# Early modulation on unsplit float32 weights, and one group of late modulation moved to the feed-forward head

## The chip, the cores and the metric

One core of a Trainium2 chip runs one launch of the kernel. The metric is device time in microseconds (us), lower is better. All inputs lie in the chip's memory (HBM); all arithmetic is on values of 32 bits.

## The reference, cut to what matters

One layer of a streaming encoder, for 512 prompt positions and 32 sample positions, 544 columns in all, with a width of 2048:

```
mod = silu(c) @ w_mod + b_mod          # 2048 x 12288 weights, two rows of c (prompt, sample)
sh_a, sc_a, gt_a, sh_f, sc_f, gt_f = split(mod, 6)
h   = rmsnorm(x, g_attn) * (1 + sc_a) + sh_a
z   = h @ w_in                         # then two kinds of attention on z
x   = x + gt_a * (concat(A, B) @ w_out)
h2  = rmsnorm(x, g_ffn) * (1 + sc_f) + sh_f
u   = causal_conv3(h2 @ w_up);  y = silu(u_gate) * u_val
x   = x + gt_f * (y @ w_down)
out = rmsnorm(x, g_final)
```

Every one of the six parts of mod has 2048 numbers for each of the two rows of c.

## The kernel before

x is held transposed, features on the 128 partitions, in 16 tiles `xT[:, kt, :]` of 128 x 544. The large products are computed from operands that are split in two parts of the type float32r: `w_hi` is a copy of a weight chunk in that type (ScalarE, `hi`, L828), `w_lo` the rest (VectorE, `lo`, L1194), and `products` (L1590 to L1592) adds three matmuls, hi x hi, hi x lo and lo x hi. A weight chunk is 128 x 1024 numbers, 512 KB. Each is loaded by a transfer of SyncE's queue into one of four slots `w_raw`, in the order of the table `STREAM`; `slot_free` makes SyncE wait until the chunk that was four places earlier in the table has been used. So all stages share one ring of four slots.

The program has these stages:

- **The early stage.** 64 chunks `("e", e)` of w_mod, 8 for each of 8 groups of 512 columns, give sh_a and sc_a, which h needs. Each chunk is split like all others; the four columns of `c_parts` (hi and lo parts of silu(c), two rows) are the stationary operand and the chunk is streamed, 4 matmuls of 512 columns for a chunk (L1564). After a group, `group_out` (ScalarE) copies its row, `group_columns` (PE, L1548) turns it into columns and `group_mod` (VectorE) adds the bias. From chunk `X_AT` = 8 on PE also transposes x (L1579, L1580), 5 transposes after each of 16 chunks. POOL squares xT (L614), VectorE sums the squares, PE sums over the partitions, and POOL then multiplies each xT tile by the reciprocal root (L627) and applies scale and shift to tiles 0 to 11 (L622); ScalarE does that for the last four tiles (L849). `h_hi` and `h_lo` split h into `x_hi` and `x_lo`. The table `NORM_AT` puts one tile's `h_hi` and `h_lo` between every second chunk's `hi` and `lo`.
- **z and attention.** 72 half slabs of z on PE, with the attention between them.
- **The output projection**, 32 halves, and at its end the second norm.
- **The feed-forward head**: the first `GRP` = 4 of 44 feed-forward tiles (`hidden` with `has_down` false, jj = 0 to 3). They have no `down` products yet. Then a **loop** over the other tiles, and a tail.

The other 64 tiles of mod (gt_a, sh_f, sc_f, gt_f) are the **late modulation**: 16 groups of 8 chunks. They use no matmul for the product: VectorE multiplies and adds for the prompt (`late_sum`, L1285, two instructions of 128 x 512 for a chunk), ScalarE multiplies for the sample (`late_mul`, L887, two) and POOL adds (`late_add`, L724, two). PE only sums over the partitions at a group's end (`late_tile`, L1601). Ten groups lie in the z stage, four (`LATE2`) in the output projection, two (`LATE3`) in the head; only gt_f, needed from the loop on, is in the head.

In the head, VectorE's order for tile jj of 1 to 3 is: `lo` of one weight chunk, two late chunks, `lo` of the second, two late chunks, the convolution of the gate half, then two `lo` for the next tile's first products. For jj = 0, four late chunks stand together after the first convolution. ScalarE starts each tile (`hidden`) with a wait for PE's first half of it (`u_done`), and only then makes that tile's third chunk's `w_hi`. Before the loop SyncE waits until all four slots are free.

Of the kernel before, what the change touches and what calls it, by code (L numbers as in the profile page):

```python
# [36 lines left out]
P = 128  # L37
# [185 lines left out]
SUM_AT = X_AT + KT + 2  # L223
LAG = NW
NORM_AT = {34 + 2 * k if k < 8 else 57 + 2 * (k - 8): k for k in range(12)}
# [5 lines left out]
LATE2 = 4 * LPG  # L231
LATE3 = 2 * LPG
# [24 lines left out]
STREAM = [("e", _e) for _e in range(EC)] + [("w", 0), ("w", 1)]  # L257
# [40 lines left out]
SC0 = EC + FC0  # L298
# [6 lines left out]
def build(nc, A, O):  # L305
# [5 lines left out]
    with ctx:  # L311
# [34 lines left out]
        c_parts = on(st0, "c_parts", [P, KT, 4], F32R)  # L346
        mod_rows = [on(st0, f"mod_rows{i}", [P, EG]) for i in range(2)]
        pair = on(st0, "pair", [P, 2])
# [90 lines left out]
        ld_c, c_hi, c_lo = sem("ld_c"), sem("c_hi"), sem("c_lo")  # L439
        e_ev, e_t, e_tev = sem("e_ev"), sem("e_t"), sem("e_tev")  # L440
# [136 lines left out]
        def _(pool):  # L577
# [14 lines left out]
            pool.wait_ge(consts, 4)  # L592
            pool.tensor_tensor(pair[0:4, :], ident[0:4, 0:2], ident[0:4, 2:4], ALU.add).then_inc(consts, 1)

# [1263 lines left out]
```

## Time and profile before

| | before |
|---|---|
| median of 3 runs | 2742.48 us (2741.48 to 2748.51) |
| profiled execution | 2740.53 us, span 2738.8 us |
| PE busy | 2592.2 us, 95% of the span |
| VectorE (DVE) busy | 1641.2 us, 60% |
| ScalarE (ACT) busy | 1010.4 us, 37% |
| GpSimd (POOL) busy | 643.4 us, 23% |
| mean granted TensorE clock | 0.976 of full speed |
| moved by DMA | 324.94 MB |

The span runs from the first to the last instruction. A busy PE is not a PE at its peak: matmuls overlap, so what one costs in a row of them is the distance from its start to the next one's start. PEld is the load of a stationary operand and lies beside PE. A granted clock of 1.00 is 2.4 GHz, of 0.50 it is 1.2 GHz. A matmul on plain float32 stands in the trace as two records, one on float32r and a transpose as one.

### The profile page before, as it was taken

Reading aid. Unit: us, or ns where it says so; the run is one execution under the profiler, and the core shown is the slowest. Engines: PE = TensorE matmul, PEld = TensorE weight load, DVE = VectorE, ACT = ScalarE, POOL = GpSimd, SP = SyncE. Lnnn points to the kernel's source line nnn. Section 1 sums busy time; section 2 is a strip of 40 time slices with the busy share of each in tenths; the row PEclk is TensorE's granted clock in tenths of the full one; section 3 lists DMA queues with packets and bytes.
Section 4 is the critical chain, followed back from the end, with each engine's and each line's share of the span. In section 5 each row is a group of like instructions: output and inputs, shape, how many; then the busy total and the mean of one; then the engine's idle time right before and its main releaser. Section 6 shows DMA issues by size and latency. Waiting matters only on the chain.

```text
span 2738.8 us, 50324 instructions
## 1 busy us (share of the span) xinstructions
PE 2592.2 (95%) x19815; PEld 2452.4 (90%) x19815; DVE 1641.2 (60%) x2890; ACT 1010.4 (37%) x2015; POOL 643.4 (23%) x534
## 2 busy tenths in 40 slices
PE   5679999999998997799999999999999999999997
PEld 2258889888988997799999999999999999999997
DVE  5889889974446887864444454445444544444454
ACT  4556666664344335432222222222222222222224
POOL 3777777771002543510000000000000000000003
PEclk8799999999999998999999999999999999999998
DMA  8766556562224663443322333232232332332331
GB/s 290 240 210 181 186 176 181 181 169 63 57 56 138 170 175 91 140 123 93 92 79 79 93 93 87 84 94 87 84 89 83 93 92 78 94 91 80 92 94 69
DMA packets 416208, 324.94 MB, mean 119 GB/s; under 512 B 44410, under 2 KB 360218, under 8 KB 414880
## 3 DMA queue, kind: packets, MB, share of 16 engines
q1 hardware_dynamic: 410032, 302.55, 37.5%
q0 software_dynamic: 5248, 14.56, 1.7%
q10 hardware_dynamic: 688, 4.47, 0.4%
q8 instruction: 169, 2.77, 0.4%
q14 instruction: 71, 0.58, 0.1%
HBM read 307.67 MB, written 14.07 MB: 117 GB/s over the span
## 4 chain that ended last, share of the span: by engine, by line
PE 77%; DVE 8%; POOL 4%; issue 4%; DMA 3%; ACT 2%; SPq 1%; ACTq 0%; POOLq 0%; DVEq 0%
PE ps L1590 24%; PE ps L1592 23%; PE ps L1591 23%; DVE late_f L1285 3%; PE ps L1679 2%; PE ps L1645 2%; DMA w_raw<-in_w_out 2%; DMA w_raw<-in_w_mod 1%; POOL oT L724 1%; POOL xT L622 1%; ACT w_hi L828 1%; DVE w_lo L1194 1%; POOL xT L627 1%; DVE oT L1285 1%; PE ps L1663 1%
## 5 line engine op out<-in xcount | busy, mean ns | idle before, releaser
L1590 PE MATMUL ps<-x_hi,w_hi 128*128 128x272 f32 x4480 | 1317.2, 294 | 45.3 <-DVE w_lo L1194 25.0
L1592 PE MATMUL ps<-x_hi,w_lo 128*128 128x272 f32 x4480 | 1302.9, 291 | 0.0
L1591 PE MATMUL ps<-x_lo,w_hi 128*128 128x272 f32 x4480 | 1292.9, 289 | 0.0
L1590 PEld LDWEIGHTS ps<-x_hi,w_hi 128*128 128x128 f32 x4480 | 849.7, 190 | 62.4 <-issue 28.1
L1591 PEld LDWEIGHTS ps<-x_lo,w_hi 128*128 128x128 f32 x4480 | 851.1, 190 | 0.0
L1592 PEld LDWEIGHTS ps<-x_hi,w_lo 128*128 128x128 f32 x4480 | 848.5, 189 | 0.0
L1194 DVE TENSOR_TENSOR w_lo<-w_raw,w_hi 128x1024 fp32r<-128x1024 f32 x432 | 546.3, 1292 | 346.8 <-ACT w_hi L828 345.8
L828 ACT ACTIVATE w_hi<-w_raw 128x1024 fp32r<-128x1024 f32 x432 | 441.8, 1056 | 745.1 <-PE ps L1592 561.6
L1591 PE MATMUL ps<-y_lo,w_hi 128*128 128x272 f32 x1408 | 407.3, 289 | 0.0
L1590 PE MATMUL ps<-y_hi,w_hi 128*128 128x272 f32 x1408 | 405.7, 288 | 0.0
L1592 PE MATMUL ps<-y_hi,w_lo 128*128 128x272 f32 x1408 | 405.0, 288 | 0.0
L783 POOL TENSOR_TENSOR ext<-cv 128x544 f32<-128x544 f32 x1 | 1.5, 1517 | 1476.2 <-ACT cv L1091 1476.2
L1041 ACT ACTIVATE ext<-ps 128x272 f32<-128x272 f32 (+2 forms) x264 | 74.0, 317 | 528.2 <-PE ps L1592 527.7
L1590 PEld LDWEIGHTS ps<-y_hi,w_hi 128*128 128x128 f32 x1408 | 265.6, 189 | 0.1
L1592 PEld LDWEIGHTS ps<-y_hi,w_lo 128*128 128x128 f32 x1408 | 264.8, 188 | 0.0
L1591 PEld LDWEIGHTS ps<-y_lo,w_hi 128*128 128x128 f32 x1408 | 264.6, 188 | 0.0
L1387 DVE SCALAR_TENSOR_TENSOR x<-ps,mod,x 128x272 f32<-128x272 f32 (+2 forms) x576 | 207.6, 400 | 92.4 <-PE ps L1592 92.3
L1431 DVE COPY ext<-cols 128x2 f32 (+1 forms) x88 | 14.9, 169 | 400.8 <-ACT ext L1041 400.8
L724 POOL TENSOR_TENSOR oT<-oT 128x512 f32<-128x512 f32 x150 | 224.3, 1495 | 31.7 <-ACT oT L887 23.8
L1285 DVE SCALAR_TENSOR_TENSOR oT<-w_raw,cs,oT 128x512 f32<-128x512 f32 x150 | 179.3, 1195 | 2.8
L724 POOL TENSOR_TENSOR late_f<-late_f 128x512 f32<-128x512 f32 x90 | 140.9, 1565 | 143.1 <-ACT late_f L887 134.3
L1285 DVE SCALAR_TENSOR_TENSOR late_f<-w_raw,cs,late_f 128x512 f32<-128x512 f32 x90 | 128.0, 1422 | 3.1
(201 smaller groups left out, 2182.6 us busy)
## 6 DMA issues: line engine op xcount, KB each, us to landing
w_raw<-in_w_mod SPq DMA_DIRECT2D x192, 512.0 KB, 4.6
w_raw<-in_w_up SPq DMA_DIRECT2D x176, 512.0 KB, 4.8
w_raw<-in_w_down SPq DMA_DIRECT2D x88, 512.0 KB, 4.4
w_raw<-in_w_in SPq DMA_DIRECT2D x56, 512.0 KB, 3.9
w_raw<-in_w_in SPq DMA_DIRECT2D x32, 256.0 KB, 3.7
w_raw<-in_w_out SPq DMA_DIRECT2D x16, 512.0 KB, 5.3
w_raw<-in_w_out SPq DMA_DIRECT2D x64, 128.0 KB, 4.0
x_transposed<-xT SPq DMA_DIRECT2D x4, 1088.0 KB, 5.9
```

What stands on the lines that cost most here:

```text
L622: ins = pool.tensor_scalar(xT[:, kt, a:a + c], xT[:, kt, a:a + c], mod[:, SC_A + kt, g:g + 1], mod[:, SH_A + kt, g:g + 1], ALU.mult, ALU.add)
L724: ins = pool.tensor_tensor(acc, late_prod(n, 0) if p == 0 and k == 1 else acc, late_prod(n, k), ALU.add)
L828: act.activation(w_hi[c % NW][:, :], w_raw[raw][:, :], ACT.Copy).then_inc(s_hi, 1)
L1041: ins = act.activation(ext[x][:, a + 2 + 2 * g:a + 2 + 2 * g + n], bank(2 * x + h)[:, a - HALF[h][0]:a - HALF[h][0] + n], ACT.Copy)
L1194: dve.tensor_tensor(w_lo[c % NW][:, :], w_raw[raw][:, :], w_hi[c % NW][:, :].bitcast(F32), ALU.subtract).then_inc(s_lo, 1)
L1285: ins = dve.scalar_tensor_tensor(out=acc_d(g), in0=w, scalar=c, in1=acc_d(g), op0=ALU.mult, op1=ALU.add)
L1387: ins = dve.scalar_tensor_tensor(out=x1[:, n, a:a + m], in0=b[:, a - HALF[h][0]:a - HALF[h][0] + m], scalar=mod[:, gate + n, g:g + 1], in1 ...
L1590: pe.matmul(out[:, 0:n], hi_w, hi_x, start=first, stop=False)
L1591: pe.matmul(out[:, 0:n], hi_w, lo_x, start=False, stop=False)
L1592: return pe.matmul(out[:, 0:n], lo_w, hi_x, start=False, stop=last)
L1645: mm = pe.matmul(S[t % 2][0:np_, pc:pc + n], zq[qi % 2][r, q0:q0 + np_], kk, start=True, stop=True)
L1679: mm = pe.matmul(B7[0:np_, oc:oc + vn], probsT[0:n, tc:tc + np_], v, start=first, stop=last)
```

## The change

In the early stage:

- The chunks of w_mod are no longer split. PE multiplies `w_raw` itself, as float32, with the two columns of `cs` = silu(c) as the stationary operand: 2 float32 matmuls of 512 columns for a chunk (4 records) in the place of 4 float32r ones. 64 `hi` and 64 `lo` fall away, and SyncE frees a slot when PE has used the chunk (`m_used`), not when `lo` has.
- `group_columns` transposes rows of 2, and no longer sums pairs of 4, one record for each of 32 tiles where there were two.
- POOL's part of the norm is gone. ScalarE squares each transposed tile out of PSUM. VectorE's `h_mul` multiplies by scale and reciprocal root in one instruction, ScalarE's `h_hi` adds the shift and writes `x_hi`, and VectorE's `h_lo` adds the shift again and subtracts `x_hi`. Each of the three has two pieces for a tile, 512 prompt and 32 sample columns.
- In `STREAM` the two first chunks of w_in stand ahead of the last two of w_mod.

In the late modulation one group of 8 chunks moves: `LATE2` falls from 4 to 3 groups and `LATE3` rises from 2 to 3. A tile of the head now has 6 late chunks instead of 4.

```diff
-SUM_AT = X_AT + KT + 2
-LAG = NW
-NORM_AT = {34 + 2 * k if k < 8 else 57 + 2 * (k - 8): k for k in range(12)}
+SUM_AT = X_AT + KT + 4
+W_AT = 62
...
-LATE2 = 4 * LPG
-LATE3 = 2 * LPG
+LATE2 = 3 * LPG
+LATE3 = 3 * LPG
...
-STREAM = [("e", _e) for _e in range(EC)] + [("w", 0), ("w", 1)]
+STREAM = [("e", _e) for _e in range(W_AT)] + [("w", 0), ("w", 1)] + [("e", _e) for _e in range(W_AT, EC)]
...
-        HEAD_LATE[_j, _q] = [LATE1 + LATE2 + 4 * _j + 2 * _q + _i for _i in range(2)]
+        HEAD_LATE[_j, _q] = [LATE1 + LATE2 + 6 * _j + 3 * _q + _i for _i in range(3)]
...
-                if old[0] != "mod":
-                    sp.wait_ge(s_lo, old[1] + 1 + (EC if old[0] == "w" else 0))
+                if old[0] == "w":
+                    sp.wait_ge(s_lo, old[1] + 1)
+                elif old[0] == "e":
+                    sp.wait_ge(m_used, old[1] + 1)
...
+            def h_hi(kt):
+
+                act.wait_ge(n_mul, kt + 1)
+                for a, c, g in ((0, TP, 0), (TP, TS, 1)):
+                    ins = act.activation(x_hi[:, kt, a:a + c], xT[:, kt, a:a + c], ACT.Identity,
+                                         bias=mod[:, SH_A + kt, g:g + 1])
+                ins.then_inc(n_hi, 1)
...
+            def h_mul(kt):
+
+                for a, c, g in ((0, TP, 0), (TP, TS, 1)):
+                    ins = dve.scalar_tensor_tensor(out=xT[:, kt, a:a + c], in0=xT[:, kt, a:a + c],
+                                                   scalar=mod[:, SC_A + kt, g:g + 1], in1=n0_rstd[:, a:a + c],
+                                                   op0=ALU.mult, op1=ALU.mult)
+                ins.then_inc(n_mul, 1)
...
+            for q in range(4):
+                for g in range(max(3, 2 * q), 2 * q + 2):
+                    if g == E_GROUPS - 1:
+                        lo(0, RAW_OF[("w", 0)] % NR, 0)
+                        lo(1, RAW_OF[("w", 1)] % NR, 1)
+                    group_mod(g)
+                dve.wait_ge(mod_ok, q + 1)
+                for kt in range(EGT * q, EGT * q + EGT):
+                    h_mul(kt)
+                    if kt >= 2:
+                        h_lo(kt - 2)
+            h_lo(KT - 2)
+            h_lo(KT - 1)
...
-                pe.wait_ge(s_lo, e + 1)
+                raw = RAW_OF[("e", e)] % NR
+                pe.wait_ge(ld_raw[raw], LOADED[("e", e)])
                 for k in range(EK):
                     kt = EK * (e % EPG) + k
-                    for part in (w_hi, w_lo):
-                        mm = pe.matmul(bank(7 - g % 2)[0:4, :], c_parts[:, kt, :], part[e % NW][:, EG * k:EG * k + EG],
-                                       start=(kt == 0 and part is w_hi), stop=(kt == KT - 1 and part is w_lo))
+                    mm = pe.matmul(bank(7 - g % 2)[0:2, :], cs[:, kt, :], w_raw[raw][:, EG * k:EG * k + EG],
+                                   start=kt == 0, stop=kt == KT - 1)
                 mm.then_inc(m_used, 1)
```

PE's queue where the transposes of x begin, before: chunk 8 of w_mod, the 5 transposes of one x tile, and the next chunk.

```order
L1564 MATMUL ps<-w_hi,c_parts 4x512
L1564 MATMUL ps<-w_lo,c_parts 4x512
L1564 MATMUL ps<-w_hi,c_parts 4x512
L1564 MATMUL ps<-w_lo,c_parts 4x512
L1579 MATMUL ps<-ident,x_nat 128x128 x4
L1580 MATMUL ps<-ident,x_nat 128x32
L1564 MATMUL ps<-w_hi,c_parts 4x512
L1564 MATMUL ps<-w_lo,c_parts 4x512
```

The same place of PE's queue after the change; the first row holds chunks 6, 7 and 8.

```order
L1539 MATMUL ps<-w_raw,cs 2x512 x6
L1556 MATMUL ps<-ident,x_nat 128x128 x4
L1557 MATMUL ps<-ident,x_nat 128x32
L1539 MATMUL ps<-w_raw,cs 2x512 x2
L1523 MATMUL ps<-ident,mod_rows 128x2 x4
L1556 MATMUL ps<-ident,x_nat 128x128 x4
```

The matmuls read the loaded chunk and wait for no split; group 0's columns are made two chunks after its end, not four.

VectorE's queue at the end of the early stage, after the change: groups 6 and 7 of mod with the two splits of w_in's first chunks between them, then the last norm tiles.

```order
L1164 TENSOR_TENSOR mod<-ps,cols 128x4 x2
L1155 TENSOR_TENSOR w_lo<-w_raw,w_hi 128x1024 x2
L1164 TENSOR_TENSOR mod<-ps,cols 128x4 x2
L1126 SCALAR_TENSOR_TENSOR mod<-mod,cols 128x4 x2
L1174 SCALAR_TENSOR_TENSOR xT<-xT,mod,n_rstd 128x512
L1174 SCALAR_TENSOR_TENSOR xT<-xT,mod,n_rstd 128x32
L1183 SCALAR_TENSOR_TENSOR x_lo<-xT,mod,x_hi 128x512
L1183 SCALAR_TENSOR_TENSOR x_lo<-xT,mod,x_hi 128x32
```

Before, four single `x_lo` instructions of 128x544 stood behind group 7; now four `h_mul` and six `h_lo`, two pieces each, stand behind it.

VectorE's queue in the head, tiles jj = 0 and 1, before:

```order
L1285 SCALAR_TENSOR_TENSOR late_f<-w_raw,cs,late_f 128x512 x7
L1194 TENSOR_TENSOR w_lo<-w_raw,w_hi 128x1024 x2
...
L1194 TENSOR_TENSOR w_lo<-w_raw,w_hi 128x1024
L1285 SCALAR_TENSOR_TENSOR late_f<-w_raw,cs,late_f 128x512 x4
L1194 TENSOR_TENSOR w_lo<-w_raw,w_hi 128x1024
L1285 SCALAR_TENSOR_TENSOR late_f<-w_raw,cs,late_f 128x512 x4
L1431 COPY ext<-cols 128x2
```

The same rows after the change:

```order
L1261 SCALAR_TENSOR_TENSOR late_f<-w_raw,cs,late_f 128x512 x11
L1155 TENSOR_TENSOR w_lo<-w_raw,w_hi 128x1024 x2
...
L1155 TENSOR_TENSOR w_lo<-w_raw,w_hi 128x1024
L1261 SCALAR_TENSOR_TENSOR late_f<-w_raw,cs,late_f 128x512 x4
L1258 TENSOR_SCALAR late_f<-w_raw,cs 128x512
L1261 SCALAR_TENSOR_TENSOR late_f<-w_raw,cs,late_f 128x512
L1155 TENSOR_TENSOR w_lo<-w_raw,w_hi 128x1024
L1261 SCALAR_TENSOR_TENSOR late_f<-w_raw,cs,late_f 128x512 x6
L1407 COPY ext<-cols 128x2
```

Four more instructions of 128 x 512 stand ahead of the `w_lo` pair that the next tile's first products wait for, in tile 0 and in every other tile of the head.

## Rows read from the trace of the kernel before

**Rows 1.** Busy time by stretch: length, PE, PEld, DVE, ACT, POOL, clock, DMA share, GB/s
```profile
88.00:174.00 86.00, 56.93 (x194) 18.95 (x192) 70.27 (x64) 48.48 (x56) 71.79 (x42) 0.81 0.74 224
856.00:1057.00 201.00, 192.73 (x1504) 190.28 (x1504) 160.56 (x185) 71.69 (x95) 91.78 (x60) 0.99 0.63 175
1097.00:1200.00 103.00, 85.07 (x659) 83.93 (x657) 86.27 (x89) 44.01 (x77) 49.07 (x30) 0.95 0.48 137
```

**Rows 2.** Groups by line, 0 to 175 us: busy, mean ns | idle before, releaser
```profile
L828 ACT ACTIVATE w_hi<-w_raw 128x1024 fp32r<-128x1024 f32 x66 | 68.3, 1051 | 53.0 <-DMA w_raw<-in_w_mod 51.3 <-DMA w_raw<-in_w_in 1.3 <-PE ps L1564 0.4
L1564 PE MATMUL ps<-w_hi,c_parts 128*4 128x512 f32 x128 | 61.6, 482 | 55.8 <-DVE w_lo L1194 55.6
```

**Rows 3.** Timeline of the norm in the early stage: start, us, engine, line
```profile
107.31 1.35 POOL L627 TENSOR_TENSOR xT<-xT,n_rstd 128x544 f32<-128x544 f32 x1
108.84 3.50 POOL L622 TENSOR_SCALAR xT<-xT,mod 128x512 f32<-128x512 f32 x2 [0.18 <-POOL xT L627]
112.31 1.36 POOL L627 TENSOR_TENSOR xT<-xT,n_rstd 128x544 f32<-128x544 f32 x1
```

**Rows 4.** Timeline, z stage: one float32 matmul of 512 columns, and what follows it
```profile
249.05 1.04 PE L1645 MATMUL ps<-past_kT,zq 64*32 64x512 f32 x2
249.93 0.22 PE L1645 MATMUL ps<-zk,zq 64*32 64x32 f32 x2
```

**Rows 5.** Timeline, the first transposes of x and the chunk behind them
```profile
38.07 0.60 PE L1579 MATMUL ps<-ident,x_nat 128*128 128x128 f32 x4
...
38.77 0.39 PE L1564 MATMUL ps<-w_hi,c_parts 128*4 128x512 f32 x1
...
39.00 0.39 PE L1564 MATMUL ps<-w_lo,c_parts 128*4 128x512 f32 x1
```

**Rows 6.** Transfers to 175 us: median us to landing of x's last; w_mod's, 90 to 120
```profile
x_nat<-in_x_sample ACTq DMA_DIRECT2D x1, 256.0 KB, 21.5
...
DMA to landing us min/median/max: 3.6/4.5/4.9
```

**Rows 7.** Timeline: last matmul of w_mod, the first of z, and the 49th of z
```profile
170.84 0.39 PE L1564 MATMUL ps<-w_lo,c_parts 128*4 128x512 f32 x1
...
174.27 0.39 PE L1590 MATMUL ps<-x_hi,w_hi 128*128 128x272 f32 x1
...
182.69 0.28 PE L1590 MATMUL ps<-x_hi,w_hi 128*128 128x272 f32 x1
```

**Rows 8.** All instructions of L1285 on `late_f`: ns min/median/max, first and last start
```profile
L1285 DVE SCALAR_TENSOR_TENSOR late_f<-w_raw,cs,late_f x90: 732/1592/1776, 859.2 to 1191.6; 128x512 f32<-128x512 f32 x90
```

**Rows 9.** Waits in the output projection, 856 to 1057 us: total, times, longest
```profile
PE ps L1590 <- DVE w_lo L1194: 6.8, 8, 2.6
```

**Rows 10.** Groups by line in the head, 1097 to 1200 us
```profile
L724 POOL TENSOR_TENSOR late_f<-late_f 128x512 f32<-128x512 f32 x30 | 49.1, 1636 | 48.1 <-ACT late_f L887 41.6 <-issue 3.7
L1285 DVE SCALAR_TENSOR_TENSOR late_f<-w_raw,cs,late_f 128x512 f32<-128x512 f32 x30 | 45.0, 1500 | 1.5
```

**Rows 11.** VectorE's timeline in the head, tiles 0 and 1
```profile
1102.73 9.97 DVE L1285 SCALAR_TENSOR_TENSOR late_f<-w_raw,cs,late_f 128x512 f32<-128x512 f32 x7
1112.62 2.35 DVE L1194 TENSOR_TENSOR w_lo<-w_raw,w_hi 128x1024 fp32r<-128x1024 f32 x2
...
1141.26 2.35 DVE L1194 TENSOR_TENSOR w_lo<-w_raw,w_hi 128x1024 fp32r<-128x1024 f32 x2
```

**Rows 12.** PE's waits at the starts of tiles 1, 2 and of the loop
```profile
1113.98 0.56 PE L1590 MATMUL ps<-x_hi,w_hi 128*128 128x272 f32 x1 [10.59 <-DVE w_lo L1194]
1142.62 0.36 PE L1590 MATMUL ps<-x_hi,w_hi 128*128 128x272 f32 x1 [1.10 <-DVE w_lo L1194]
1200.23 0.59 PE L1590 MATMUL ps<-x_hi,w_hi 128*128 128x272 f32 x1 [2.71 <-DVE w_lo L1194]
```

**Rows 13.** ScalarE's timeline: third weight chunk of tiles 1 and 2
```profile
1121.82 1.06 ACT L828 ACTIVATE w_hi<-w_raw 128x1024 fp32r<-128x1024 f32 x1 [2.90 <-PE ps L1592]
...
1148.91 1.06 ACT L828 ACTIVATE w_hi<-w_raw 128x1024 fp32r<-128x1024 f32 x1 [1.35 <-PE ps L1592]
```

More of the change, by code:

```diff
@@ L345, in build @@
         lam = [on(st0, f"lambda{i}", [P, A_DK]) for i in range(4)]
-        c_parts = on(st0, "c_parts", [P, KT, 4], F32R)
-        mod_rows = [on(st0, f"mod_rows{i}", [P, EG]) for i in range(2)]
-        pair = on(st0, "pair", [P, 2])
+        mod_rows = [on(st0, f"mod_rows{i}", [2, EG]) for i in range(2)]
         rows = on(st0, "rows", [P, 9, P])
@@ L871, in _ @@
                     act.wait_ge(lam_dot, 2)
                     act.activation(tiny[:, 4:6], tiny[:, 6:8], ACT.Exp).then_inc(lam_exp, 1)
-                if e == SUM_AT + LAG:
-                    root(0, n0_rstd[:, :])
-                if e in NORM_AT:
-                    h_hi(NORM_AT[e])
+            group_out(2)
+            root(0, n0_rstd[:, :])
+            for kt in range(EGT):
+                h_hi(kt)
+            group_out(3)
+            for kt in range(EGT, 2 * EGT):
+                h_hi(kt)
@@ L877, in late_mul @@
+            group_out(4)
+            group_out(5)
+            for kt in range(2 * EGT, 3 * EGT):
+                h_hi(kt)
+            group_out(6)
+            hi_early(0)
+            hi_early(1)
+            group_out(7)
+            for kt in range(3 * EGT, KT):
+                h_hi(kt)
             def late_mul(n):
@@ L1246, in _ @@
-            lo(0, RAW_OF[("w", 0)] % NR, EC)
-            lo(1, RAW_OF[("w", 1)] % NR, EC + 1)
-            group_mod(E_GROUPS - 1)
-            for kt in range(len(NORM_AT), KT):
-                h_lo(kt)
+                for a, c, g in ((0, TP, 0), (TP, TS, 1)):
+                    ins = dve.scalar_tensor_tensor(out=x_lo[:, kt, a:a + c], in0=xT[:, kt, a:a + c],
+                                                   scalar=mod[:, SH_A + kt, g:g + 1],
+                                                   in1=x_hi[:, kt, a:a + c].bitcast(F32), op0=ALU.add, op1=ALU.subtract)
@@ new lines, in h_lo @@
+                ins.then_inc(x_ok, 1)
+            dve.wait_ge(rows_t, len(ROW_COUNTS))
+            for i in range(1, len(ROW_COUNTS)):
+                row_out(i)
+            dve.wait_ge(ld_small, 80)
+            for i in range(2):
+                a, b = lam[2 * i], lam[2 * i + 1]
+                dve.tensor_tensor_reduce(a[:, :], a[:, :], b[:, :], 1.0, 0.0, ALU.mult, ALU.add,
+                                         tiny[:, 6 + i:7 + i]).then_inc(lam_dot, 1)
+            dve.wait_ge(rows_ev, len(ROW_COUNTS))
@@ new lines, in _ @@
+            group_mod(0)
+            for kt in range(1, KT):
+                dve.wait_ge(sq_mul, kt + 1)
+                if kt > 1:
+                    dve.wait_ge(sq_add, kt - 1)
+                ins = dve.tensor_tensor(n0_acc[:, :], n0_sq[0][:, :] if kt == 1 else n0_acc[:, :],
+                                        n0_sq[kt % 2][:, :], ALU.add)
+                ins.then_inc(sq_ok if kt == KT - 1 else sq_add, 1)
+            dve.wait_ge(lam_exp, 1)
+            step(dve.tensor_tensor(tiny[:, 3:4], tiny[:, 5:6], tiny[:, 4:5], ALU.subtract))
@@ L1546, in group_columns @@
                 for t in range(EGT):
[L1547 to L1549 removed]
+                    mm = pe.transpose(bank(5)[:, 2 * t:2 * t + 2], mod_rows[g % 2][0:2, P * t:P * t + P],
+                                      ident[0:2, 0:2])
                 mm.then_inc(e_t, 1)
[L1553 removed]
             for e in range(EC):
```

148 lines of the change are left out of this document (34 added, 114 removed).

## The prediction

> **What bounds the kernel now.** I read the busy time by stretch first, then for each stretch the change touches its groups and timeline. In the early stage nothing is full: from 88 to 174 us PE is busy 57 of 86 us at a granted clock of 0.81, and DMA moves 224 GB/s [rows 1]. PE waits 55.6 us for `w_lo` and ScalarE 51.3 us for weights [rows 2]. The releasers hide the cause. POOL needs 5.0 us for one tile of the norm, from one L627 to the next (107.31 to 112.31), and is never free in between [rows 3]. `NORM_AT` sets one tile against two chunks, and ScalarE and VectorE work in order; so over the 12 tiles that POOL scales, a chunk costs 2.5 us whatever DMA and PE could do.
>
> In the output projection PE is the bound, 192.7 of 201 us busy [rows 1], with 6.8 us of waits for `w_lo` [rows 9]. In the head it is not: 85.1 of 103 us busy, beside VectorE with 86.3 [rows 1]. 45.0 us of those are the 30 late instructions L1285 [rows 10], and tiles 1, 2 and the loop each start with PE waiting for a `w_lo`: 10.59, 1.10 and 2.71 us [rows 12]. What stands ahead of that `w_lo` in VectorE's queue are the late chunks [rows 11]. From the loop on PE is full, so a microsecond lost or won ahead of it stays.
>
> **Early stage: the chunks.** A float32 matmul of 512 columns costs 0.88 us at full clock, from 249.05 to 249.93 [rows 4]. The new chunk has two: 1.76 us, against four float32r ones of 0.23 (38.77 to 39.00 [rows 5]), 0.92. So PE's own work on the 64 chunks rises from 59 to 113 us, but the split, its waits and POOL's pace go. That row has 32 stationary columns and 64 rows, ours 2 and 128; I take the same price, since the number of streamed columns is the same. The five transposes of a tile of x take 0.70 us (38.07 to 38.77 [rows 5]).
>
> The start stays: the sample part of x lands 21.5 us after its issue at about 4 us [rows 6], and DMA is full until then. Both kernels should have used chunk 8 at about 38 us, where the first transposes of x stand now [rows 5]. From there the sum is 55 chunks x 1.76 = 96.8 us, 16 x 0.70 = 11.2, the sum of squares and 7 groups of columns about 5 (my estimate; the parts are 4 transposes each). That gives 151 us for the last matmul on w_mod, if PE never waits. DMA must give 512 KB in 1.76 us, about 298 GB/s; a slot's transfer lands in 4.5 us, and a slot has 3 x 1.76 = 5.3 us until PE is back [rows 6]. That holds by a small margin, so I add 4 us for waits and drops of the clock: 155 us, bounds 151 and 165, against 171.1 now (170.84 and one matmul [rows 7]). Squares and copies on ScalarE and the sums on VectorE lie beside this; a tile of x and a chunk leave them 2.46 us, and with POOL silent they have their short durations.
>
> **Early stage: the end.** Now z starts 3.4 us after the last matmul on w_mod and its first half of 48 matmuls ends at 182.7 us [rows 7]. The four last `x_lo` were short single instructions. After the change z can start at once, but `x_ok` for tiles 10 to 15 lies behind group 7's scale: copy, 4 transposes and the small sums 2.2 us, then four `h_mul` and six `h_lo` on VectorE. The minimum of L1285, two inputs and 512 columns, is 0.73 us [rows 8], which I read as the price without POOL's adds beside it; with the 32-column piece I take 0.95, an estimate. That is 2.2 + 9.5 + 0.4 = 12.1 us, longer than the matmuls of the half. So the first half of z ends at 155 + 12 = 167 us against 182.7: **15 us won**, with bounds 5 and 20. The 68 us of splits that ScalarE is rid of [rows 2] are no further gain: they lie beside PE's longer matmuls.
>
> A rule of the Trainium skill speaks against this. The row first: at 38.77 us, between two sets of transposes, the 512-column matmuls stand 0.23 us apart [rows 5], which is 2.4 GHz. "TensorE: Matmul & The Clock Gate", in "Part 4: PE-mode transpose", says that transposes do not count as work for the clock and that the full clock does not engage for them. By the row the stretch of 16 tiles costs 16 x 2.46 = 39 us; by the rule, taken for the whole stretch, it would run at 1.2 GHz and cost 78. The row decides here, as matmuls are most of the stretch.
>
> **Late modulation.** The moved group has 8 chunks, each with two instructions on VectorE, ScalarE and POOL, and one transfer on SyncE's queue. In the output projection these lay beside PE's products. What they give back is at most the 6.8 us of waits [rows 9] and part of ScalarE's and the gaps of `late_tile`; I take **3 us**, bounds 0 and 8.
>
> In the head they are on the path. Tile 0: seven L1285 take 9.97 us, then two `w_lo`, and PE starts at 1113.98 [rows 11, 12]. Two more chunks stand ahead of that. Tiles 1 to 3: the chain is PE's start, its first half, ScalarE's third chunk (1121.82 for tile 1 [rows 13]), `w_lo`, late chunks, `w_lo`, late chunks, convolution, the next `w_lo` pair, PE's start. It closes in 28.64 us, 1113.98 to 1142.62 [rows 12], where PE needs 192 matmuls and about 24. The slack of PE on this chain is the 1.10 us it waits; the work that hid the late chunks is used up. So every added chunk lengthens each tile by its time on VectorE: 2 x 1.5 = 3.0 us at the mean of the head [rows 10]. Two a tile, four tiles: 8 x 3.0 = 24 us. POOL does not set this, 6 x 2 x 1.64 = 19.7 us in a tile [rows 10]; nor ScalarE or DMA. Before the loop SyncE waits for all slots, and this wait moves by the same two chunks.
>
> Longer gaps also cool PE. From PE's start to the third chunk's `w_hi` tile 1, after a gap of 10.59 us, takes 7.84 us, tile 2, after 1.10 us, 6.29 [rows 12, 13]. That is 1.5 us for a cold start; I add it for two of the tiles, 3 us. **27 us lost.** Bounds: below 16 x 0.73 = 11.7 us, if each late instruction ran as without POOL [rows 8]; above 16 x 1.78 = 28.4 and a cold start at two places in each of four tiles, 6 x 1.5 more, 38. I take a value near the mean because POOL's adds run at the same time as now.
>
> **The sum**, against the profiled execution: 2740.5 - 15 - 3 + 27 = 2749.5 us. It lies 2 us under the median of the runs, so for a median 2751.5, rounded to 2752.
>
> **Rivals.** What a measurement can tell from no change here is about 0.3%, 8.2 us: slower begins at 2750.7, faster ends at 2734.3.
>
> 1. *The head takes the chunks more cheaply, no change.* With 18 us won ahead, the head must cost between 10 and 26 us, 1.2 to 3.3 us a chunk. For it: my sum without cold starts, 24 us, is already in this band. Against: the waits get longer, and chunks back to back meet POOL more often. Time at 20 us: 2744.
> 2. *The head has room, faster.* VectorE is busy 86 of 103 us [rows 1]; if its idle 17 us took most of the added 24, the head would cost 7 us and the result be 2731. It decides below 10 us, 1.2 us a chunk, and even the bare VectorE time at its minimum, 11.7, is above that, unless the early stage wins 20. Against: the idle time stands where VectorE waits for ScalarE's third chunk, which waits for PE, and the order is fixed.
> 3. *The early stage wins little.* A ring of four slots that cannot keep 298 GB/s, as now with 224 [rows 1], gives 2.05 us a chunk: 40 chunks x 0.29 = 12 us back, net +21, 2764. For it: only 0.8 us of margin in a slot's time.
> 4. *The clock falls to 1.2 GHz while x is transposed*: the stretch of 39 us takes twice that, 2791. For it: a granted clock of only 0.81 in the stretch behind it now [rows 1]; against: the 0.23 us between the matmuls at its start [rows 5]. The rule of the Trainium skill named above ("TensorE: Matmul & The Clock Gate") would give this result.
>
> **How the numbers follow.** The forecast as summed (net +5 to +18) 0.50; rival 1 0.23; rival 2 0.12; rival 3 0.12; rival 4 0.03. A third of the first case's lower end falls under 0.3%, so slower is 0.36 + 0.12 + 0.03, about 0.51, the same 0.36, faster 0.13. The range leaves out rival 4, most of rival 2 and the end of rival 3: 2738 to 2766. The forecast's own range is 2747 to 2760.
>
> **What the profile after would show.** Records of the w_mod matmuls 0.43 us apart, four a chunk, and the clock near 1.00 from 88 us on; the last of them at 151 to 165 us; PE waiting for `x_lo` in the first half of z, which ends near 167. In the output projection fewer waits and an end 18 us earlier than now, 1038. In the head three starts of tiles 34 us apart where it is 28 to 30 now, PE waiting some 16 us for tile 1, and a second wait of 4 us in the middle of each tile; the loop's start near 1209 where it is 1200.2. Behind it, nothing changed. It would be wrong if late instructions in the head fell toward 0.73 us, if PE's pitch on w_mod were not 0.43, or if transfers of 512 KB took over 5.3 us.

## The result and the profile after

The change makes the kernel slower by 0.4%: 2751.95 us median (2748.78 to 2757.23, 18 runs) against 2742.67 us (2735.64 to 2748.85, 18 runs of the kernel before on the same chip), ratio 1.0039 with a 95% interval of 1.0031 to 1.0046. The forecast was 2752.

The profiled execution after took 2757.23 us (span 2755.5), the longest of its 18 runs and 5.3 us over their median; the one before took 2740.53, 2.1 us under its own. So the two traces differ by 16.7 us and the medians by 9.3. What follows shows where the 16.7 lie; how much of a stage is stable is shown by kernels that share it.

The stages by PE's queue, in us: start of the 49th matmul of z; from there to the start of the output projection's third half (its first two halves stand among the last attention pieces); from there to the first matmul of the head; the head, to the first matmul of the loop; and the loop. These five are differences of start times in the two traces.

| | 49th of z | rest of z | output projection, norm | head | loop |
|---|---|---|---|---|---|
| before | 182.7 | 673.7 | 213.3 | 130.6 | 1460.2 |
| after | 169.8 | 675.9 | 201.3 | 159.0 | 1471.1 |
| difference | -12.9 | +2.2 | -12.0 | +28.4 | +10.9 |

Busy time by stretch of the kernel after, which answers to [rows 1]: length, PE, PEld, DVE, ACT, POOL, clock, DMA share, GB/s.

```profile
88.00:158.00 70.00, 64.69 (x158) 12.63 (x157) 25.83 (x59) 16.05 (x31) 0.00 (x0) 0.95 0.87 282
846.00:1034.00 188.00, 186.67 (x1488) 186.14 (x1486) 133.93 (x163) 60.40 (x77) 65.92 (x45) 1.00 0.60 164
1074.00:1206.00 132.00, 96.01 (x678) 94.96 (x677) 111.31 (x108) 55.38 (x93) 72.25 (x45) 0.85 0.48 139
```

The early stage now belongs to PE (64.7 of 70 us) and DMA (282 GB/s where it was 224), with POOL silent. The output projection has no gap left (186.7 of 188). In the head PE is busy 96 of 132 us, and the clock fell to 0.85.

The early stage, groups by line to 160 us, answering to [rows 2], and the transfers from 90 to 120 us, answering to [rows 6]:

```profile
L1539 PE MATMUL ps<-w_raw,cs 128*2 128x512 f32 x256 | 124.0, 632 | 14.0 <-DMA w_raw<-in_w_mod 13.2 <-ACT cs L786 0.7
```

```profile
w_raw<-in_w_mod SPq DMA_DIRECT2D x16, 512.0 KB, 4.7
```

PE's timeline in that stage, answering to [rows 5, 7]: the 4 records of a chunk in 1.81 us with the transposes behind them, then the last chunks and the start of z.

```profile
41.25 1.88 PE L1539 MATMUL ps<-w_raw,cs 128*2 128x512 f32 x4
43.06 0.66 PE L1556 MATMUL ps<-ident,x_nat 128*128 128x128 f32 x4
...
152.37 6.54 PE L1539 MATMUL ps<-w_raw,cs 128*2 128x512 f32 x8 [3.94 <-DMA w_raw<-in_w_mod]
...
159.91 0.40 PE L1565 MATMUL ps<-x_hi,w_hi 128*128 128x272 f32 x1
...
165.66 0.40 PE L1565 MATMUL ps<-x_hi,w_hi 128*128 128x272 f32 x1 [0.96 <-DVE x_lo L1183]
...
169.80 0.43 PE L1565 MATMUL ps<-x_hi,w_hi 128*128 128x272 f32 x1
```

One wait of 3.94 us stands ahead of chunk 62: in `STREAM` two chunks of w_in are ahead of it, and it shares their ring. The last matmul of w_mod starts at 158.3. Behind the wait the granted clock is 1.2 GHz, and the last two chunks take 6.5 us, where two take 3.6 at full clock:

```profile
151.50:158.30 6.80, 5.93 (x8) 0.85 (x8) 1.23 (x1) 0.64 (x1) 0.00 (x0) 0.50 0.82 235
```

VectorE's timeline behind group 7, the chain that ends z's first half:

```profile
160.56 0.92 DVE L1174 SCALAR_TENSOR_TENSOR xT<-xT,mod,n_rstd 128x512 f32<-128x512 f32 x2
161.39 0.91 DVE L1183 SCALAR_TENSOR_TENSOR x_lo<-xT,mod,x_hi 128x512 fp32r<-128x512 f32 x2
...
166.34 2.56 DVE L1183 SCALAR_TENSOR_TENSOR x_lo<-xT,mod,x_hi 128x512 fp32r<-128x512 f32 x6
```

A piece pair starts 0.83 us behind the one ahead of it; ten take 8.3 us, and the last `x_lo` ends at 168.9.

Waits of PE in the output projection, 846 to 1034 us, answering to [rows 9]; then the head's groups by line, 1074 to 1206 us, answering to [rows 10]:

```profile
PE ps L1565 <- DVE w_lo L1155: 1.8, 2, 1.3
```

```profile
L696 POOL TENSOR_TENSOR late_f<-late_f 128x512 f32<-128x512 f32 x45 | 72.2, 1606 | 53.3 <-ACT late_f L860 45.1 <-issue 3.6 <-POOL late_f L696 0.3
L1261 DVE SCALAR_TENSOR_TENSOR late_f<-w_raw,cs,late_f 128x512 f32<-128x512 f32 x45 | 67.4, 1499 | 2.4
```

VectorE's late instructions kept their mean (1500 before, 1499 now) and became 45 from 30. Where this shows on PE, its starts of tiles 1, 2 and 3, the middle of tile 3, and the start of the loop, answering to [rows 12]:

```profile
1098.09 0.57 PE L1565 MATMUL ps<-x_hi,w_hi 128*128 128x272 f32 x1 [17.28 <-DVE w_lo L1155]
1133.31 0.37 PE L1565 MATMUL ps<-x_hi,w_hi 128*128 128x272 f32 x1 [0.34 <-DVE w_lo L1155]
1167.45 0.36 PE L1565 MATMUL ps<-x_hi,w_hi 128*128 128x272 f32 x1
1188.97 0.46 PE L1565 MATMUL ps<-x_hi,w_hi 128*128 128x272 f32 x1 [4.67 <-DVE w_lo L1155]
1206.04 0.60 PE L1565 MATMUL ps<-x_hi,w_hi 128*128 128x272 f32 x1 [4.51 <-DVE w_lo L1155]
```

The tiles start 35.2 and 34.1 us apart. All that was read ahead. What was not is the loop. PE's timeline at its first back edge, before and then after; the release named is "issue", nothing that the profile shows:

```profile
1494.98 0.39 PE L1590 MATMUL ps<-x_hi,w_hi 128*128 128x272 f32 x1 [2.40 <-issue]
```

```profile
1500.92 0.59 PE L1565 MATMUL ps<-x_hi,w_hi 128*128 128x272 f32 x1 [3.56 <-issue]
```

The distance from the last matmul of a pass to the first of the next is 2.68, 1.99, 1.99 and 2.08 us at the four back edges before, and 3.85, 2.97, 3.73 and 3.63 after: 5.4 us together. Behind each of the four gaps of after the granted clock falls to 1.2 GHz for a while, behind those of before only once, behind the longest; that is 20.5 us in all against 3.4. The same matmuls then keep PE busy for 1458.0 us of the loop where it was 1452.4, 5.6 us more. The 5.4 and the 5.6 make up the 10.9. The nine us behind the second edge, before and then after:

```profile
1788.00:1797.00 9.00, 9.00 (x72) 9.00 (x73) 1.60 (x2) 2.29 (x3) 0.00 (x0) 1.00 0.02 5
```

```profile
1796.00:1805.00 9.00, 9.00 (x60) 9.00 (x61) 0.09 (x1) 1.18 (x2) 0.00 (x0) 0.81 0.02 5
```

The same nine us hold 72 matmuls before and 60 after, at a clock of 1.00 and 0.81.

### The profile page after: what moved, and what is told of

It is laid out like the page before. It is cut to its first block, busy times and chain, and to the rows that moved or that the text cites. A ratio compares the mean times of both kernels' runs of the same rounds, so it can differ in the third digit from the quotient of the medians.

```text
span 2755.5 us, 50104 instructions
## 1 busy us (share of the span) xinstructions
PE 2635.4 (96%) x19783; PEld 2457.6 (89%) x19783; DVE 1555.3 (56%) x2871; ACT 957.8 (35%) x1974; POOL 541.8 (20%) x477
## 4 chain that ended last, share of the span: by engine, by line
PE 86%; DVE 6%; issue 2%; POOL 2%; DMA 2%; ACT 1%; ACTq 0%; SPq 0%; DVEq 0%; POOLq 0%
PE ps L1565 25%; PE ps L1567 25%; PE ps L1566 25%; PE ps L1539 4%; DVE late_f L1261 2%; PE ps L1654 2%; PE ps L1620 2%; DMA w_raw<-in_w_mod 1%; POOL oT L696 1%; PE ps L1638 1%; PE ps L1576 1%; DVE oT L1261 1%; DVE w_lo L1155 1%; PE ps L1663 0%; DMA w_raw<-in_w_out 0%
## 5 line engine op out<-in xcount | busy, mean ns | idle before, releaser
L1155 DVE TENSOR_TENSOR w_lo<-w_raw,w_hi 128x1024 fp32r<-128x1024 f32 x368 | 458.5, 1275 | 341.6 <-ACT w_hi L798 341.3
L798 ACT ACTIVATE w_hi<-w_raw 128x1024 fp32r<-128x1024 f32 x368 | 375.4, 1056 | 722.9 <-PE ps L1567 582.2
L696 POOL TENSOR_TENSOR oT<-oT 128x512 f32<-128x512 f32 x150 | 224.0, 1493 | 32.1 <-ACT oT L860 23.8
L696 POOL TENSOR_TENSOR late_f<-late_f 128x512 f32<-128x512 f32 x90 | 138.2, 1535 | 154.0 <-ACT late_f L860 144.1
L1539 PE MATMUL ps<-w_raw,cs 128*2 128x512 f32 x256 | 124.0, 632 | 14.0 <-DMA w_raw<-in_w_mod 13.2
```

The costliest lines, as they stand in the source:

```text
L696: ins = pool.tensor_tensor(acc, late_prod(n, 0) if p == 0 and k == 1 else acc, late_prod(n, k), ALU.add)
L798: act.activation(w_hi[c % NW][:, :], w_raw[raw][:, :], ACT.Copy).then_inc(s_hi, 1)
L1155: dve.tensor_tensor(w_lo[c % NW][:, :], w_raw[raw][:, :], w_hi[c % NW][:, :].bitcast(F32), ALU.subtract).then_inc(s_lo, 1)
L1539: mm = pe.matmul(bank(7 - g % 2)[0:2, :], cs[:, kt, :], w_raw[raw][:, EG * k:EG * k + EG], start=kt == 0, stop=kt == KT - 1)
```

## The experiments

They were run in three batches, in which the median of the kernel before was 2741.8, 2740.2 and 2741.8 us; each ratio is to the kernel before in its own batch. Times of different batches, set against each other, can be off by these 1 to 2 us.

**Each part alone.** First the early stage as changed, with the groups as before (10 in z, 4 in the output projection, 2 in the head):

```diff
-LATE2 = 3 * LPG
-LATE3 = 3 * LPG
+LATE2 = 4 * LPG
+LATE3 = 2 * LPG
```

> The changed early stage alone, with the late modulation placed as in the kernel before (LATE2 of 4 groups, LATE3 of 2). Theory A (the parts are independent; the early part wins 12 to 13 us up to z, the rest runs as before): 2742.6 - 12.5 = 2730 us, 2726 to 2735, with z's second half starting near 176.8 us, the output projection's length as before (200 us), the loop starting near 1188 us. Rival B (the shorter output projection came with the early part and not with the moved group): 2720. Rival C (PE's time at the loop's back edge, 3.0 to 3.9 us where it was 2.0 to 2.7, comes from the early part's shorter instruction stream): 2735 to 2740, with edges of 3 us or more.

Measured: 2736.14 us, ratio 0.9980 (0.9970 to 0.9991). The 49th matmul of z starts at 165.9, the loop 15.4 us earlier than before, and the loop then takes 1470.4 us. Theory A's 2730 missed; rival C has the time and the edges, 3.0 to 3.8 us.

Then the early stage as before, with one group moved:

```diff
-LATE2 = 4 * LPG
-LATE3 = 2 * LPG
+LATE2 = 3 * LPG
+LATE3 = 3 * LPG
```

> The moved group alone on the kernel before. Theory A: the head (first products of the feed-forward to the loop) costs 27 to 29 us more, the output projection gives back 9 to 10: 2742.6 + 18 = 2761 us, 2757 to 2765, with the back edges of the loop as before, 2.0 to 2.7 us. Rival B (the projection gives nothing without the early part): 2770. Rival C (the edges become longer with the moved group): 2765 to 2770 with edges of 3 us or more.

Measured: 2755.1 us, ratio 1.0051 (1.0036 to 1.0067). Output projection and norm 202.3 us, head 158.5, loop 1459.9. The parts add up: -5.6 and +13.3 give +7.7, the change measured +9.3. The time lies under theory A's range, but its parts came: 27.9 us in the head, 11.0 back from the projection, edges of 1.8 to 2.6 us. The slower loop comes with the early stage, over 1000 us ahead of it, and the head's loss with the group.

**Where the group could go.** Starting from the changed kernel, the group moved into z (11, 3, 2), and another one from the head into the output projection (10, 5, 1):

```diff
-LATE1 = 10 * LPG
-LATE3 = 3 * LPG
+LATE1 = 11 * LPG
+LATE3 = 2 * LPG
```

> The changed kernel, but the moved group stands in the z stage (LATE1 of 11 groups, LATE2 of 3, LATE3 of 2), none more in the head than before. Theory A (VectorE is busy about 500 of 682 us in z, so 8 more chunks of 3 us are hidden there, while the projection keeps its gain of 10 us): 2742.6 - 12.5 - 10 + 3 = 2723 us, 2719 to 2729. Rival B (in z too VectorE is the bound in places and the group costs half of its 24 us): 2732 to 2736.

```diff
-LATE2 = 3 * LPG
-LATE3 = 3 * LPG
+LATE2 = 5 * LPG
+LATE3 = 1 * LPG
```

> The changed early stage with the late modulation moved the other way: LATE2 of 5 groups, LATE3 of 1. Theory A (in the head each chunk lies on VectorE's path down to PE's 24 us a tile, so the head wins about 20 us against the kernel before; the projection, with VectorE then busy some 183 of 201 us, loses about 15): 2742.6 - 12.5 - 20 + 15 = 2725 us. Rival B (the projection becomes bound by VectorE and loses 25 or more): 2735 to 2740.

Measured: 2733.11 us for the first, ratio 0.9965 (0.9952 to 0.9977), and 2759.73 for the second, 1.0064 (1.0049 to 1.0079). The first has rival B's time, but not for its reason: z took about 7 us more, not 12, and the rest is the slower loop (1472.2 us). The second missed both theories. The second's output projection, 841 to 1082 us, by stretch, and PE's waits in it:

```profile
841.00:1082.00 241.00, 206.55 (x1516) 202.98 (x1517) 185.88 (x202) 81.52 (x110) 112.27 (x75) 0.93 0.56 163
```

```profile
PE ps L1565 <- DVE w_lo L1155: 26.6, 15, 7.2
```

PE waits 26.6 us for `w_lo` where it waited 1.8: five groups fill what three or four had left free.

**What makes a late chunk dear in the head.** The changed kernel, with POOL's additions of the late chunks in the head on one column of 512. It leaves out that part of gt_f's sums for the sample; everything else runs as it was.

```diff
                 for k in range(1 if p == 0 else 0, LK):
-                    ins = pool.tensor_tensor(acc, late_prod(n, 0) if p == 0 and k == 1 else acc, late_prod(n, k),
-                                             ALU.add)
+                    c = slice(0, 1) if n >= LATE1 + LATE2 else slice(0, LG)
+                    ins = pool.tensor_tensor(acc[:, c], (late_prod(n, 0) if p == 0 and k == 1 else acc)[:, c],
+                                             late_prod(n, k)[:, c], ALU.add)
```

> The changed kernel, in which POOL's adds of the late chunks in the head take one column instead of 512, so the sample rows of gt_f are not summed in full. Nothing else moves. Theory A (VectorE's time for a late chunk, about 3 us because POOL's adds run beside it, sets the head): L1261 in the head falls from 1.5 us toward 0.73, a chunk costs 1.5 us, tile 1 starts about 9 us earlier and each of the three tiles falls from 34 to 38 us to 25 or 26, close to PE's own 24; from the first product of the head to the loop 159 us become 120 to 128. Rival B (the transfers, ScalarE's copies or the one wait of SyncE set it): 145 us or more.

Measured: 2715.39 us in one run. Groups of the head, 1067 to 1165 us:

```profile
L1262 DVE SCALAR_TENSOR_TENSOR late_f<-w_raw,cs,late_f 128x512 f32<-128x512 f32 x45 | 33.9, 753 | 3.4 <-DMA w_raw<-in_w_mod 1.0
L697 POOL TENSOR_TENSOR late_f<-late_f 128x1 f32<-128x1 f32 x45 | 21.9, 486 | 70.6 <-ACT late_f L861 64.1 <-issue 3.6 <-POOL late_f L697 0.2
```

The same 45 instructions of VectorE now take 753 ns each, not 1499, and the head takes 125.1 us, not 159.0: less than the 130.6 of the kernel before, with one group more in it. PE starts tiles 2 and 3 and the loop without a wait, 28.4, 26.9 and 26.8 us apart. So a chunk's 3 us of VectorE are half POOL's doing, and the chain over `w_lo` was it that set the head. The edit also takes away ScalarE's waits for POOL (22.0 us in the head of the changed kernel, 1.4 here). These did not lie on the chain: with them VectorE works without a gap from tile 1's third chunk (1108.04 us) to the `w_lo` pair that tile 2 waits for. A late instruction near 0.73 us was what the prediction named as its lower bound; it takes POOL's silence to get there.

**Was POOL what paced the early stage before?** The kernel before, with scale and shift (L622) of the 12 tiles moved to ScalarE; POOL keeps only the 16 multiplications L627.

```diff
-                if kt < 2 * EGT:
-                    scale_shift(kt)
-            for kt in range(2 * EGT, 3 * EGT):
-                scale_shift(kt)
...
+                if e + 1 in NORM_AT:
+                    scale_shift(NORM_AT[e + 1])
                 if e in NORM_AT:
                     h_hi(NORM_AT[e])
```

> The kernel before, in which ScalarE applies scale and shift to all 16 tiles of the first norm (one chunk earlier than the split of the tile) and POOL only multiplies by the reciprocal root; the weights stay split. Theory A (POOL's 5.0 us for a tile set the pace of the second half of the early stage, not the splits): z starts 10 us or more earlier than 174.3, 2742 falls to 2729 to 2734. Rival B (the splits on ScalarE and VectorE are the bound, and unsplit weights were needed for the gain): z starts within 4 us of 174, time the same.

Measured: 2743.57 us, ratio 1.0007 (0.9996 to 1.0018); the 49th matmul of z 2.5 us earlier. POOL's timeline, and the two stretches behind the norm's root:

```profile
95.70 31.34 POOL L627 TENSOR_TENSOR xT<-xT,n_rstd 128x544 f32<-128x544 f32 x15
```

```profile
97.00:122.00 25.00, 15.37 (x41) 4.49 (x42) 24.97 (x16) 16.33 (x23) 25.00 (x13) 0.64 0.58 169
122.00:162.00 40.00, 29.88 (x100) 8.30 (x99) 32.15 (x34) 29.56 (x40) 6.07 (x5) 0.79 0.83 264
```

With nothing between them the multiplications run back to back at 2.09 us each, and VectorE, 24.97 of 25 us busy beside them, gets 16 instructions done: chunks 32 to 40 take 25.0 us where they took 17.2. Then POOL falls silent, and chunks 40 to 60 take 39.3 us where they took 48.1; ScalarE now waits for transfers (12.6 us in this second stretch). So POOL did set the pace of chunks 40 to 60, but behind it stood a second limit at 2.0 us, and of the 8.8 us won there 7.8 were lost ahead of it. The time is rival B's; its reason, that the splits alone are the bound, is not what the two stretches show.

Which of POOL's instructions slow VectorE can be read from the kernel before, beside scale and shift (the L622 at 108.84 of [rows 3]) and then beside the multiplications of tiles 8 to 15:

```profile
109.17 2.35 DVE L1194 TENSOR_TENSOR w_lo<-w_raw,w_hi 128x1024 fp32r<-128x1024 f32 x2
...
137.20 16.89 POOL L627 TENSOR_TENSOR xT<-xT,n_rstd 128x544 f32<-128x544 f32 x8
139.05 13.82 DVE L1194 TENSOR_TENSOR w_lo<-w_raw,w_hi 128x1024 fp32r<-128x1024 f32 x6
```

Of the 24 `w_lo` that lie wholly beside L622, which has one input tile, 20 take 1.21 to 1.23 us, the same as with POOL silent (1.21 to 1.23 in the run above, after 128 us); the other four take 1.57 to 1.72. The six beside L627, which has two input tiles, take 2.36 to 2.38. So it is not POOL's mere presence that doubles VectorE's time in these traces; beside its instructions with two input tiles it doubles, and L696 of the head is one of these too. The change took out all of POOL's work and the splits together; whether one of the two would have been enough with L627 gone as well was not tried.

**The loop.** The counts of PE's instructions ahead of the loop are 16012 before and 15948 after, 64 fewer (32 matmuls of the columns and their weight loads). To test whether that alone slows the loop, the kernel with 11, 3 and 2 groups got 32 unused transposes of 32 x 32 ahead of the head's second tile, 64 instructions, and the kernel before got 96 of them, 192 instructions:

```diff
+            for _ in range(32):
+                pe.transpose(bank(7)[0:32, 0:32], ident[0:32, 0:32], ident[0:32, 0:32])
             for jj in range(1, GRP):
```

> The kernel with the group in z (2733.1 us), with 32 small transposes of the identity into an unused bank ahead of the head's tile 1, where PE waits anyway. They bring PE's count of instructions ahead of the loop back to that of the kernel before, 64 more. Theory A (the early change shortened PE's stream by 64 instructions, so the loop's first instruction lies otherwise in the blocks in which instructions are fetched, and the back edge waits for one fetch more): edges fall from 3.6 to 2.0 to 2.7 us, the loop from 1472 to 1460 us, the time to 2723. Rival B (the edges depend on something else, as the order of the transfers): 2733, edges as they are.

> The kernel before with 96 small transposes, 192 instructions, ahead of the head's tile 1, inside PE's wait of 10.6 us. Theory A (fetch blocks of 256 instructions, so that 192 more are the same place in a block as 64 fewer): edges rise from 2.0 to 2.7 us to 3.0 to 3.9, the time from 2742 to 2752. Rival B (the place in a block does not matter): 2742, edges as before.

Measured: 2721.07 us with 64 more, 12.0 us less than without them, ratio 0.9927 (0.9914 to 0.9941) to the kernel before; and 2753.16 us for the kernel before with 192 more, ratio 1.0040 (1.0027 to 1.0054). Both are what theory A said. The loops take 1459.1 and 1471.2 us. The second's back edge, and the queue q8, which carries blocks of instructions, in the 8 us ahead of the edge (packets, MB, share), first in the kernel before (1487 to 1495 us), then before with 192 more (1484.8 to 1492.8), then after (1493 to 1501):

```profile
1492.79 0.59 PE L1590 MATMUL ps<-x_hi,w_hi 128*128 128x272 f32 x1 [3.33 <-issue]
```

```profile
q8 instruction: 1, 0.02, 0.8%
```

```profile
q8 instruction: 2, 0.03, 2.8%
```

```profile
q8 instruction: 2, 0.03, 2.9%
```

Each is a block of 16 KB. One took 0.97 us, at 1492.36 of the kernel before; the two of the changed kernel, at 1496.54 and 1496.57, took 1.85 and 1.89. The traces of all fourteen kernels of this document fall into the same two kinds. Eight have 16012 instructions ahead of the loop: one block ahead of each edge, gaps of 1.6 to 3.1 us (mean 2.2), loops of 1458.7 to 1461.7 us. The five with 15948 and the one with 16204 have two blocks side by side, gaps of 3.0 to 3.9 us (mean 3.5), loops of 1468.7 to 1472.2. That 192 added to the kernel before does the same as 64 taken away fits a period of 256 instructions: 16012 + 192 and 15948 leave the same remainder by 256. The Trainium skill, "Runtime: NRT & Kernel Launch", "Instruction fetch mechanics", says that instructions are fetched in blocks of 16 KiB, which are 256 instructions, and that a taken branch whose target is not at hand forces a fetch before work goes on; this case's trace agrees, with one block at the edge and 1.6 to 3.1 us, or two and 3.0 to 3.9. Which instructions of the edge lie across a block's border was not tried, and no other remainder than these two.

Last the change itself, with the 64 instructions given back:

> The changed kernel with 64 more instructions in PE's queue ahead of the loop (32 transposes of 32 x 32 before the head's second tile, results unused), as many as the change took away. Theory A: the 10.9 us that the loop lost hang on where the loop's code lies, and on nothing else that the change did. Then PE's gaps at the four back edges are 2.0 to 2.7 us again, the loop takes 1460 us and not 1471, and the time is some 2752 - 11 = 2741 us, no change against the kernel before: 13 won in the early stage, 10 in the output projection, 28 lost in the head, and the rest a few us for the padding and drifts. Theory B: the loop is slower because of the state in which the new early stage and head leave it (transfers late, clock); then the gaps stay at 3 to 4 us and the time at 2750 or above.

Measured: 2738.84 us (11 runs), ratio 0.9990 (0.9980 to 0.9999). 13.1 us less than the change without them; the loop takes 1461.3 us and the blocks at its edge are one again, with gaps of 1.6 to 3.1 us. This is theory A, with two of the four gaps (2.8 and 3.1) above its 2.7. The early stage (49th of z at 168.8) and the head (158.5) are as in the change.

**Better allotments.** On the kernel at 2721.07: w_in's first two chunks behind w_mod's last one (against PE's wait of 3 to 4 us for chunk 62), then instead one more group from the head to z (12, 3, 1), then both.

```diff
-W_AT = 62
+W_AT = 64
...
             hi_early(0)
-            hi_early(1)
             group_out(7)
+            hi_early(1)
...
-                        lo(1, RAW_OF[("w", 1)] % NR, 1)
                     group_mod(g)
+                    if g == E_GROUPS - 1:
+                        lo(1, RAW_OF[("w", 1)] % NR, 1)
```

> The kernel with a group in the z stage and 64 more instructions on PE (2721.1 us), with the first two chunks of w_in placed behind the last chunk of w_mod in the order of transfers, not ahead of the last two; ScalarE and VectorE split the first of them ahead of group 7's modulation and the second behind it. PE waits 3 to 4 us for chunk 62 of w_mod, since two other chunks stand ahead of it in the ring. Theory A: that wait is what the early stage of the change missed; without it the last matmul on w_mod starts near 151 us where it was 154.7 and the 49th matmul of z at 163 where it was 166.1, so the time is 2718 us. Theory B: the wait only moves: w_in's first chunk now comes after 152 us, z starts no earlier than 156, and its first half ends at 166 or later; the time is 2721 or more.

> The kernel with 64 more instructions on PE, and one more group of late modulation moved, from the head to the z stage: 12 groups in z, 3 in the output projection, 1 in the head (the kernel at 2721.1 us has 11, 3, 2). Theory A: a place has a price for each group: some 8 to 11 us in z, as the first group there cost, against 17.7 us that the head takes for its second one (131.0 us from the head's first product to the loop with two groups, 113.3 with one). The net is 7 to 10 us faster, about 2713 us. Theory B: z is filled up: a ring that already moves two chunks more for each half slab delays w_in, and the second group there costs over 18 us; the time is 2721 or above.

> Both of the two edits before this one together: 12, 3 and 1 groups, and w_in's first chunks behind w_mod's last. If both give what theory A expects of them, 3 and 8 us, and do not meet, the time is 2710 us; if the transfers meet at z's start, where late chunks begin in the third half slab, it is nearer to the better of the two alone, about 2713.

Measured: 2720.16 us (0.9917, 0.9902 to 0.9932), 2742.75 (1.0001, 0.9988 to 1.0014) and 2743.96 (1.0006, 0.9995 to 1.0018). PE's timeline for the first:

```profile
142.74 10.46 PE L1540 MATMUL ps<-w_raw,cs 128*2 128x512 f32 x24
154.67 0.41 PE L1524 MATMUL ps<-ident,mod_rows 2*128 2x2 f32 x4 [1.47 <-ACT mod_rows L818]
155.45 0.40 PE L1566 MATMUL ps<-x_hi,w_hi 128*128 128x272 f32 x1 [0.38 <-DVE w_lo L1155]
```

The wait on the transfer is gone, and most of its time turns up as later waits: for the group's copy, `w_lo` and `x_lo`. The 49th matmul of z starts at 166.4, where it was 166.1: theory B, within a us. For the second, PE's longest waits in z, 176 to 880 us:

```profile
PE ps L1654 <- ACT oT L901: 18.2, 15, 2.3
```

The kernel with eleven groups waits 1.7 us there. Theory B has the time, but PE waits for ScalarE's `oT` and not for w_in, and why `oT` comes late was not tried. In the trace the twelfth group costs z 33 us and wins 18 in the head, 15 us net; that execution (2735.1) lies 7.7 us under the median of its ten runs, so by medians it is 22. Both edits together missed both numbers of their forecast. All runs together give each place its price, from the same differences of starts as the first table (the range over all kernels with that number of groups there, in the head without the one whose additions were cut):

| groups in the stage | z from its 49th matmul | output projection, norm | head |
|---|---|---|---|
| fewest | 10: 671.9 to 675.9 | 3: 200.7 to 204.1 | 1: 113.3 to 114.7 |
| one more | 11: 680.5 to 682.2 | 4: 213.1 to 214.8 | 2: 129.4 to 131.7 |
| two more | 12: 713.3 to 715.3 | 5: 254.8 | 3: 158.5 to 159.0 |

Each column bends upwards: by the means, the next group costs 7 and then 33 us in z, 12 and then 41 in the output projection, 17 and then 28 in the head. Of the splits that were run, 11, 3 and 2 is the best. The table itself points at one that was not: with 11, 4 and 1 the projection would pay 12 us and the head give back 17, an estimate of 5 us less. With its 64 instructions the kernel with 11, 3 and 2 runs at 2721 us, 0.7% faster than the kernel before, and the variant with `W_AT` = 64 cannot be told from it.

## Why the prediction was right, and where it was not

The time, 2752, was right; the sum behind it was not in all its terms. With the loop's fetches as they were, the change is worth -3.0 us by medians (2738.84 against 2741.84) and +2.9 by the two profiled executions (2743.43 against 2740.53); the sum had +9. The loop's edges, of which it knew nothing, brought 13.1 by medians. The sum was 6 to 12 us too high ahead of the loop and 11 to 13 too low behind it, so that the total came out within 1 us is luck. Without the loop's part the result would have been the no-change case of rival 1, and not for that rival's reason, since the head cost more than rival 1 allows.

- **Early stage, -15 us (5 to 20).** Measured -12.9 in the change, and -13.9 to -16.8 in the kernels that share its early stage unchanged. The pitch of 0.43 us, the transfers' 4.5 to 4.7 us and the full clock on the transposes came as read: 1.00 from 37 to 88 us in the kernel after. The clock rule of the Trainium skill ("TensorE: Matmul & The Clock Gate", "Part 4: PE-mode transpose") did not show here; this stretch is mostly matmuls, so it says little on transposes alone. The 4 us for waits and clock were too few: of the 14.0 us of idle time ahead of L1539 most lie ahead of chunk 8, but the 3.94 at chunk 62 and the 3 us that the clock behind it cost are 7. The end was a little shorter than summed: 11.1 us from the last matmul on w_mod (158.7) to the 49th of z, not 12.1. Rival 3 fell (282 GB/s, and one long wait for a transfer), rival 4 with the clock of 1.00.
- **The pace by POOL** was half true. POOL took 5.0 us a tile for tiles 0 to 7 only, not for all 12; then came the eight multiplications from 137 to 154 us, beside which a `w_lo` takes 2.36 us. It paced chunks 40 to 60, but a second limit stood close behind, as the run with ScalarE's scale and shift shows. It entered no term of the sum.
- **Output projection, -3 us (0 to 8).** Mis-sized: the projection with the norm gave -12.0, and 11.0 in the kernel with that part alone. PE's waits for `w_lo` fell from 6.8 to 1.8 us; `late_tile` of one group, 16 matmuls on PE, is gone with some 2 us (64 of them are 7.9 us busy in the kernel with four groups, overlapped starts); and the 3.4 us at 1.2 GHz that followed the longest gap of before (2.9 us from start to start) are gone too (up to 1.7 us): 0.99 became 1.00. Those are some 9 of the 12 us; most of the rest lies in shorter gaps. The step that failed is "these lay beside PE's products": a full engine pays for matmuls that a late group issues, and a gap can cost more than its length.
- **Head, +27 us.** Measured +28.4, with tiles 35.2 and 34.1 us apart (34), a wait of 17.3 us for tile 1 (16), 4.5 to 4.7 us in the middle of each tile (4), and a mean of 1499 ns for VectorE's instruction (1500). Its cause is shown from the other side: without POOL's additions the head falls to 125.1 us. Rivals 1 and 2 fell with it.
- **"Behind it, nothing changed"** is the step that was wrong: the loop took 10.9 us more. No engine's work changed behind the head, but the place of PE's code did, and with it the cost of every back edge. The diff's one record for each of 32 column tiles where there were two was counted in the early stage and nowhere else.

## What to carry to other kernels

Background work has a marginal price in every stage, not a mean: measure the next piece in each place and fill up where it is lowest; a stage that charged 7 us for its eleventh group charged 33 for the twelfth. When an edit changes PE's instruction count ahead of a loop, look at the back edges' gaps and the instruction queue, and try a few dozen idle instructions, before the rest of the difference is explained. For an engine on the critical chain, ask what durations it would have without its neighbour, and which of the neighbour's instructions cost it: here POOL's additions, with POOL busy only half of the head, doubled VectorE's.

## What the runs showed of the hardware that was not expected

- PE's back edge took 1.6 to 3.1 us with one block of 16 KB fetched and 3.0 to 3.9 us with two, which hung on 64 instructions ahead of the loop; with the drops of the clock behind them the second block costs the loop 10 to 13 us of 2750.
- Short gaps cost clock as well. In the kernel with twelve groups in z the granted clock was 1.2 GHz for 20.5 us between 270 and 600 us, and never in the one with ten; up to 10 of the 33 us are that.
- VectorE's two-input instruction of 128 x 512 took 753 ns with POOL's additions cut to a column and 1499 ns beside them; `w_lo`, two inputs of 128 x 1024, took 2.36 us beside POOL's multiplications of two tiles and 1.21 beside its scale and shift of one. POOL's multiplications paid too: 1.34 to 1.36 us for tiles 1 to 7 in the kernel before, and 2.3 beside a row of `w_lo`.
